# Two transformer blocks on one core: the router fed by the raw residual, and a new order of splits in the third block

## What is computed

```python
def memory_cross_attention(h, mem_n, ...):        # 4 heads of 256
    q = rms_norm_2((h @ w_cq).reshape(B, S, X_HEADS, X_HEAD_DIM), cq_norm)
    k = rms_norm_2((mem_n @ w_ck).reshape(B, M, X_HEADS, X_HEAD_DIM), ck_norm)
    v = (mem_n @ w_cv).reshape(B, M, X_HEADS, X_HEAD_DIM)
    p = jax.nn.softmax(scores, axis=-1)
...
def hierarchical_moe(h, w_router_group, w_router_expert, w1, w3, w2):
    p_group = jax.nn.softmax(xf @ w_router_group, axis=-1)     # 4 groups
    g_idx = jnp.argmax(p_group, axis=-1)
    local = jnp.einsum('td,gde->tge', xf, w_router_expert)     # 8 experts per group
    top_logit, top_idx = lax.top_k(local of the group, 2)
    gate = jax.nn.softmax(top_logit, axis=-1) * g_w[:, None]
    hid = jax.nn.silu(xblk @ w1[e]) * (xblk @ w3[e]); y = hid @ w2[e]    # 32 experts
...
    x = x + mixed @ w_out                          # mixed: window attention (8 heads) and a spatial gate
    x = x + memory_cross_attention(rms_norm_2(x, norm_cross), mem_n, ...)
    x = x + hierarchical_moe(rms_norm_2(x, norm_ffn), ...)
```

## Time and profile before

| | us |
|---|---|
| median of three executions | 1487.49 (1486.2 to 1488.25) |
| the profiled execution's own time | 1483.92 |
| span of the profile | 1481.9 |
| PE busy | 1437.8 (97%) |
| DVE busy | 755.2 (51%) |
| ACT busy | 565.2 (38%) |
| mean granted TensorE clock | 0.986 of full speed |

### The profile page before, as it was taken

One profiled execution on the slowest core, in us unless ns is written; L12 is line 12 of the kernel. 1 busy time (PEld: TensorE's weight loads), 2 busy tenths in 40 slices (PEclk: granted clock), 3 DMA queues, 4 the chain that ended last, 5 costly groups with the idle time before them and its releaser, 6 DMA issues. The chain is left out here.

```text
span 1481.9 us, 26323 instructions
## 1 busy us (share of the span) xinstructions
PE 1437.8 (97%) x11240; PEld 1211.5 (82%) x11240; DVE 755.2 (51%) x1194; ACT 565.2 (38%) x885; POOL 28.6 (2%) x47
## 2 busy tenths in 40 slices
PE   7999999999999999999999899999999999999997
PEld 4998899999999879999999789888666566566664
DVE  3968767876776656555555655644122122122121
ACT  2522235343454555444444664451212212212211
POOL 0100000000001010000000000010000000000000
PEclk9999999999999999999999999999999999999999
DMA  9996455979769514665645336426999999999996
GB/s 370 309 322 211 155 174 196 328 279 319 280 225 327 177 52 164 207 222 204 210 132 168 118 114 236 163 62 253 413 424 427 425 427 425 428 427 425 426 425 263
DMA packets 155378, 404.14 MB, mean 273 GB/s; under 512 B 5107, under 2 KB 123152, under 8 KB 133906
## 3 DMA queue, kind: packets, MB, share of 16 engines
q1 hardware_dynamic: 152960, 396.90, 71.1%
q0 software_dynamic: 1648, 5.18, 1.2%
q10 hardware_dynamic: 674, 0.64, 0.1%
HBM read 401.63 MB, written 1.07 MB: 272 GB/s over the span
## 5 line engine op out<-in xcount | busy, mean ns | idle before, releaser
L1999 PE MATMUL ps<-u,wsplit 128*128 128x256 f32 x3744 | 461.7, 284 | 5.3 <-DVE wsplit L1268 5.3
L1999 PEld LDWEIGHTS ps<-u,wsplit 128*128 128x128 f32 x3744 | 452.8, 192 | 11.9 <-DVE wsplit L1268 6.4
L1268 DVE TENSOR_TENSOR wsplit<-arena,wsplit 128x1024 fp32r<-128x1024 f32 x258 | 312.5, 1226 | 198.7 <-ACT wsplit L807 198.5
L807 ACT ACTIVATE wsplit<-arena 128x1024 fp32r<-128x1024 f32 x258 | 270.1, 1056 | 294.9 <-PE ps L1999 150.8
L2666 PE MATMUL ps<-arena 128*64 128x256 f32 x1408 | 155.9, 379 | 1.1 <-DVE arena L1897 0.8
L2666 PEld LDWEIGHTS ps<-arena 128*64 128x64 f32 x1408 | 101.6, 137 | 60.8 <-issue 12.6
L1902 DVE TENSOR_TENSOR arena<-arena,ps 128x256 f32<-128x256 f32 x32 | 13.5, 422 | 235.9 <-ACT arena L1216 223.8
L2261 PE MATMUL ps<-hid,wsplit 128*128 128x256 f32 x1056 | 130.7, 283 | 0.3 <-DVE hid L1524 0.3
L2261 PEld LDWEIGHTS ps<-hid,wsplit 128*128 128x128 f32 x1056 | 128.3, 192 | 0.5 <-DVE hid L1524 0.5
L1221 ACT ACTIVATE arena<-ps 64x512 f32<-64x512 f32 x62 | 36.6, 591 | 141.4 <-PE ps L2688 140.7
L2045 PE MATMUL ps<-wsplit,u 128*128 128x256 f32 x672 | 83.2, 284 | 1.8 <-ACT arena L1074 1.6
(11 more groups left out here) (369 smaller groups left out, 1376.3 us busy)
## 6 DMA issues: line engine op xcount, KB each, us to landing
arena<-in_w SPq DMA_DIRECT2D x64, 2048.0 KB, 22.4
late<-in_w SPq DMA_DIRECT2D x30, 2048.0 KB, 23.5
arena<-in_mod_w SPq DMA_DIRECT2D x48, 1024.0 KB, 7.0
arena<-in_ffn_w_in SPq DMA_DIRECT2D x44, 1024.0 KB, 5.9
arena<-in_ffn_w_out SPq DMA_DIRECT2D x22, 1024.0 KB, 5.0
arena<-in_a_w_in SPq DMA_DIRECT2D x16, 1024.0 KB, 8.6
arena<-in_kv_mod_w SPq DMA_DIRECT2D x8, 1024.0 KB, 4.9
arena<-in_kv_w SPq DMA_DIRECT2D x8, 1024.0 KB, 7.2
```

The source lines that it names most:

```text
L807: act.activation(piece_buf(p, 0), piece_src(p), ACT.Copy).then_inc(hi_done, 1)
L1268: dve.tensor_tensor(piece_buf(p, 1), piece_src(p), piece_buf(p, 0).bitcast(F32), ALU.subtract).then_inc(lo_done, 1)
L1999: mm = pe.matmul(o, w_[:, k, :], u[:, x_, k, :], start=first, stop=last)
```

## The change

Three things are altered.

1. **Router.** The router's weights go to `late`, 64 columns to a chunk (36 used, the rest zero), and are multiplied by the norm's weights on DVE (`m_gain`) between two steps of `co`. PE multiplies them by the raw residual, even chunks into partitions 0 to 63 of bank 6 and odd ones into 64 to 127 (`raw_logits`). DVE copies the sums to `log_t`, and PE adds the two halves and turns them by token in one product with `unite` (a doubled identity). DVE multiplies the 36 logits of each token by its reciprocal root.
2. **Tokens.** The scaled chunks and the permuted identity are gone. The residual is turned once, into banks 2 to 5, and stays there; ACT reads it from there, scales by the root and writes the tokens for the gather. The norm's weights (`token_gain`) are applied where DVE brings gathered tokens from PSUM to `xe`: a copy becomes a product.
3. **Order in the third block.** ACT writes the memory operand ahead of two of its other steps. In W, ACT goes head by head with one `between_w` behind each, and DVE puts a split between the steps of a pair. Three reciprocals of `key_norm` move into the additions of `out2`. In X, DVE does head 2's `probs` ahead of head 3's maxima and splits `co`'s pieces one by one.

The places on which the prediction rests, as each engine's instructions stand in the two kernels:

The diff, cut to its core:

```diff
+        wr = late[:, RING * SLOT:RING * SLOT + 64 * DC].rearrange("p (k e) -> p k e", k=DC)
+        token_gain = late[:, RING * SLOT + 512:RING * SLOT + 512 + DC]
+        unite = late[:, RING * SLOT + 520:RING * SLOT + 520 + NGROUP + NE]
+        log_t = late[:, RING * SLOT + 560:RING * SLOT + 560 + T]
...
-            pool.wait_ge(at_lo, 12)
-            pool.memset(turned, 0.0).then_inc(m_const, 1)
...
+            pool.wait_ge(at_s, HB + HW + HX)
+            pool.memset(wr, 0.0).then_inc(m_uni, 1)
+            pool.memset(unite, 0.0).then_inc(m_uni, 1)
+            pool.wait_ge(m_uni, 2)
...
+            pool.dma_start(token_gain, norm_ffn_2.rearrange("(p k) -> p k", k=DC)).then_inc(m_wr, 16)
...
+            pool.wait_ge(at_lo, 12)
...
+                    for i in range(n + 3):
+                        if i < n:
+                            exps(i)
+                        if 2 <= i < n + 2:
+                            copy(i - 2)
+                        if i >= 4 and i % 2 == 0:
+                            drain(i - 3)
+                        if i >= 1:
+                            between(i - 1)
...
                 hi_upto(min(FILL[0]["w"] + filled(min(i - 1, HW)) + 3, LAST["cv"] + 2))
-                while 2 * drained[0] + 2 <= min(filled(min(i - 1, HW)), 14):
+                while 2 * drained[0] + 2 <= min(filled(min(max(i - 1, 0), HW)), 14):
...
+                        hi_upto(pair[0]["w"] + LOOKAHEAD)
+                        memory_hi(pair[1]["w"])
...
+            def memory_hi(after):
...
+                act.wait_ge(x_tc, 2)
+                for c_ in range(DC):
+                    act.activation(u[:, 0, c_, :], memT[:, c_, :], ACT.Copy, scale=vec("norm_mem_2", c_))\
+                        .then_inc(u_hi, 1)
...
             in2_act()
-            wait_out(act, jobs["in2"][-1])
-            act.wait_ge(x_tc, 2)
-            for c_ in range(DC):
-                act.activation(u[:, 0, c_, :], memT[:, c_, :], ACT.Copy, scale=vec("norm_mem_2", c_)).then_inc(u_hi, 1)
...
+                    hi_upto(FILL[3]["w"])
+                    wait_out(act, jobs["in2"][-1])
...
+            act.wait_ge(rstd_done, STATS["moe"] + 1)
...
                 act.activation(
                     hn_tok[:, b, :].rearrange("p (k c q) -> p k c q", k=DC, c=DC),
-                    ps[:, 2 + 2 * b:4 + 2 * b, :].rearrange("p j (c k q) -> p k (j c) q", c=DC // 2, k=DC), ACT.Copy)\
-                    .then_inc(m_tokc, 1)
+                    ps[:, 2 + 2 * b:4 + 2 * b, :].rearrange("p j (c q k) -> p k (j c) q", c=DC // 2, k=DC), ACT.Copy,
+                    scale=stat[:, 4 + b:5 + b]).then_inc(m_tokc, 1)
...
+                    if job == "co" and n == 3:
+                        dve.wait_ge(m_wr, 96)
+                        routed = wr[:, :, 0:NGROUP + NE]
+                        gains = vec2[:, VEC["norm_ffn_2"]:VEC["norm_ffn_2"] + DC].rearrange("p (k o) -> p k o", o=1)
+                        dve.tensor_tensor(routed, routed, gains.to_broadcast([P, DC, NGROUP + NE]), ALU.mult)\
+                           .then_inc(m_gain, 1)
...
+                    if job == "out2" and n < 3:
+                        key_norm(n)
...
-                        if i == 1:
+                        if i in (1, 2):
                             probs(i)
...
-                        if i < n and i != 1:
+                        if i < n and i not in (1, 2):
...
+                    for j in range(n // 2):
+                        scores(2 * j)
+                        scores(2 * j + 1)
+                        if j == 0:
+                            split_first()
+                        probs(2 * j)
+                        if j > 0:
+                            between(2 * j - 1)
+                        probs(2 * j + 1)
+                        between(2 * j)
...
-            lo_upto(LAST["in2"] + LOOKAHEAD)
+            lo_upto(FILL[1]["w"])
...
+                    lo_upto(FILL[3]["w"])
...
+            attention_dve("W", None, between_w, lambda: lo_upto(FILL[2]["w"]))
...
                 lo_upto(p["w"] + LOOKAHEAD)
-                key_norm(n)
+                if n < 3:
+                    key_norm(3 + n)
...
-                lambda i: lo_upto(jobs["co"][(1, 3)[i]]["w"]) if i < 2 else None)
+                lambda i: lo_upto(jobs["co"][1 + i]["w"]) if i < 3 else None)
...
-            norm_rstd("moe")
-            for c_ in range(DC):
-                dve.scalar_tensor_tensor(out=sq[:, c_, :], in0=h[:, c_, :], scalar=vec("norm_ffn_2", c_), in1=rbc,
-                                         op0=ALU.mult, op1=ALU.mult).then_inc(m_hn, 1)
...
+            dve.wait_ge(bc_done, STATS["moe"])
...
+            dve.wait_ge(m_log, 1)
+            dve.tensor_copy(log_t, ps[:, 6, 0:T]).then_inc(m_log, 1)
...
-            dve.wait_ge(m_log, 1)
-            step(dve.tensor_copy(logits, ps[:, 6, 0:72].rearrange("p (b e) -> p b e", b=TB)))
...
+            step(*[dve.tensor_scalar(logits[:, b, :], ps[:, 6, T + 36 * b:T + 36 * (b + 1)], stat[:, 4 + b:5 + b], None,
+                                     ALU.mult) for b in range(TB)])
...
-                dve.tensor_copy(xe[:, 4 * half:4 * half + 4, :].rearrange("p k s -> p (k s)"), ps[:, 6 + half, :])\
-                    .then_inc(m_x, 1)
+                gains = token_gain[:, 4 * half:4 * half + 4].rearrange("p (k o) -> p k o", o=1)
+                dve.tensor_tensor(xe[:, 4 * half:4 * half + 4, :], ps[:, 6 + half, :].rearrange("p (k s) -> p k s", k=4),
+                                  gains.to_broadcast([P, 4, 2 * CAP]), ALU.mult).then_inc(m_x, 1)
...
+            def raw_logits(k):
+
+                half_ = 64 * (k % 2)
+                return pe.matmul(ps[half_:half_ + 64, 6, 0:T], wr[:, k, :], h[:, k, :], start=(k < 2), stop=(k >= DC - 2),
+                                 skip_group_check=True)
...
+            def residual(b, some):
+
+                for c_ in some:
+                    mm = pe.matmul(ps[:, 2 + 2 * b + c_ // 4, P * (c_ % 4):P * (c_ % 4 + 1)],
+                                   h[:, c_, P * b:P * (b + 1)], ident[:], start=(c_ % 4 == 0), stop=False,
+                                   skip_group_check=True)
+                if some[-1] == DC - 1:
+                    mm.then_inc(m_tok, 1)
...
+            pe.wait_ge(m_gain, 1)
+            for k in range(6):
+                raw_logits(k)
+            sums("moe", [3])
+            raw_logits(6)
+            raw_logits(7).then_inc(m_log, 1)
+            residual(0, range(2))
+            pe.wait_ge(m_log, 2)
+            pe.wait_ge(m_uni, 4)
+            for b in range(TB):
+                mm = pe.matmul(ps[:, 6, T + 36 * b:T + 36 * (b + 1)], log_t[:, P * b:P * (b + 1)], unite,
+                               start=True, stop=True, skip_group_check=True)
+            mm.then_inc(m_log, 1)
+            residual(0, range(2, DC))
+            residual(1, range(DC))
             warm(jobs["co"][4:], 3)
...
-            spread("moe")
...
-            for k in range(DC):
-                pe.wait_ge(m_hn, k + 1)
-                for b in range(TB):
-                    mm = pe.matmul(ps[:, 6, 36 * b:36 * (b + 1)], sq[:, k, P * b:P * (b + 1)], wr[:, k, :],
-                                   start=(k == 0 and b == 0), stop=(k == DC - 1), skip_group_check=True)
...
-            for b in range(TB):
-                for c_ in range(DC):
-                    mm = pe.matmul(ps[:, 2 + 2 * b + c_ // 4, P * (c_ % 4):P * (c_ % 4 + 1)],
-                                   sq[:, c_, P * b:P * (b + 1)], turned, start=c_ % 4 == 0, stop=c_ % 4 == 3)
-                mm.then_inc(m_tok, 1)
...
-            residual(0)
...
-            residual(1)
```

More of the change, by code:

```diff
@@ L608, in two_blocks @@
         slot_no = part(17920, 4, 2 * CAP)
-        wr = part(18432, DC, NGROUP + NE)
+        wr = late[:, RING * SLOT:RING * SLOT + 64 * DC].rearrange("p (k e) -> p k e", k=DC)
+        token_gain = late[:, RING * SLOT + 512:RING * SLOT + 512 + DC]
+        unite = late[:, RING * SLOT + 520:RING * SLOT + 520 + NGROUP + NE]
+        log_t = late[:, RING * SLOT + 560:RING * SLOT + 560 + T]
+        m_uni = sem("m_uni")
+        m_gain = sem("m_gain")
         logits = part(18720, TB, NGROUP + NE)
@@ L617, in two_blocks @@
         flag = part(19408, 4)
-        turned = part(17664, P)
         slot_i = part(19456, 4 * 2 * CAP)
@@ L1631, in attention_dve @@
                             drain(i - 2)
+                        between(i)
+                    return
+                if kind == "W":
+                    for j in range(n // 2):
[8 more added lines that the diff above has]
+                        between(2 * j)
+                    for i in (n - 1, n, n + 1):
                         between(i)
@@ L1751, in between_w @@
                 if i == 0:
+                    lo_upto(FILL[3]["w"])
+                    wait_out(dve, jobs["in2"][-1])
                     dve.wait_ge(w_std, 3)
```

45 lines of the change are left out of this document (20 added, 25 removed).

## The result

| | before | changed |
|---|---|---|
| median as first measured (4 executions each) | 1486.85 (1479.72 to 1488.25) | 1464.34 (1461.89 to 1465.26) |
| ratio, 95% interval | | 0.9856 (0.9822 to 0.9889) |
| the same kernel measured again | 1486.07 (9 executions) | 1466.51 (4), ratio 0.9865 (0.9849 to 0.9882) |
| mean of all executions timed with the experiments below | 1482.5 (83), mean clock 0.987 | with the first four: 1464.9 (8), mean clock 0.991 |
| span of the profile | 1481.9 | 1463.5 |

The change makes the kernel faster by 18 to 20 us, 1.2 to 1.4%: by the means over everything 1482.5 - 1464.9 is 17.7 (before rounding), by the means of the nine and four executions that ran side by side 19.6, by the medians 19.6 and 22.5. I had forecast 12.85, and 1474.6 with 1469.0 as the low end. The direction was right, the size was not.

A forecast was written before the change was run, and what follows sets the result against it. PE sets the pace before the experts, weights within them, so the end hangs on expert 0's start. 4.1 + 4.85 + 0.8 + 3.1 = 12.85 off 1483.92, plus 3.57 to the median: 1474.6 us, range 1469.0 to 1481.5.

The forecast's parts named there:

- What bounds the kernel: Weights pace the experts, PE the rest; time saved before expert 0 moves the end one to one, behind it 0.
- Window attention: Third block: earlier memory operand and splits shorten PE's pauses; 4.1 us after 1.5 off for one clock fall, bounds 1.5 to 6.0.
- Scores: Cross-attention: earlier keys' scaling removes the 1.89 pause, and 16 products take 3.8 instead of 6.76; 4.85 us.
- Turn of head 2: Cross-attention: division first cuts the wait from 2.13 to 1.4, half clock behind it kept; 0.8 us, bounds 0 and 2.6.
- Router: Logits 4.2 us sooner, 0.4 from the residual, less 1.5 for a half-clock gather; 3.1 us, bounds 2.2 and 5.2.
- The base: Sum taken from the profiled execution, 1483.92 us, with 3.57 added at the end to reach the median.
- The clock stays up everywhere: Rival: remaining pauses, 1.4 us or shorter, leave PE's clock up; gain 17.7, 1469.8. Gains above 15.5 got 0.17.
- Returned waits: Rival: window attention's pairs wait longer, scores gain only their pause; gain 7.3, 1480.2. Gains of 3 to 10 got 0.29.
- the change does what it says: Rival denied it: loads pace the query loop's split, so scores stay put; gain 8.0, 1479.5. Gains of 3 to 10: 0.29.
- Slower: Rival: odd heads' copies over 3 us late at four window attention outputs; 16 lost, +7 net, 1494; chance 0.04.
- GpSimd: Fills and selections moved beside divisions of heads 1 and 2: counted 0; by the skill's contention, sum some 0.5 us smaller.

The follow-up runs named there:

- e2: Kernel before with only three reciprocals of the keys' norm moved into the additions of out2: mean 1478.7 (12 executions), ratio 0.9968.
- e3: Kernel before with only head 2's division ahead of head 3's maxima and co's pieces split one by one: mean 1478.0 (12 executions), ratio 0.9970.
- e8: Kernel before with only window attention's memory operand and third and fourth split moved ahead, loops still by pairs of heads: mean 1478.1 (12), ratio 0.9975.
- e4: Kernel before with only the router and the tokens changed: mean 1479.3 (12 executions), ratio 0.9973.
- e12: Kernel before with four filling-product calls in the 1.89 us pause ahead of cross-attention's scores: mean 1480.1 (12) beside 1482.5 (23), ratio 0.9980.
- e6: Changed kernel with three filling products ahead of each of window attention's two gates: 121.74 us from the start of the third block to out2.
- e13: Changed kernel with ACT's split of co's fourth piece behind head 2's exponentials, plus one filler call ahead of each gate: 120.21 us from block start to out2.

## Why the prediction was off

*What bounds the kernel* was right: the end hangs on expert 0's start, the half of the residual taken from behind it gave nothing, and the pauses that were named and the router are where the time came from. The time came out 10 us lower than forecast. About 5 of that is the base, some 4 are the four terms, and two steps in them failed: what I gave back in window attention, and the price of the half clock, which I read off one profile at every place.

*Window attention, 4.1 forecast, 7.4 measured.* Of the terms this one failed most. Up to the gates the walk was right: 3.0 forecast, and they stand 63.11 us behind the start of the block instead of 66.09. Then I gave back 0.45 for the drains, 1.0 at the first outputs and 0.6 at the copies; none of these came, and the pauses alone gave 6.4 in place of 4.2 (5.6 less the 1.4 of clock in it). The remaining 1.0 is clock. I expected it to fall once as before. It does, but in four of the six old profiles it falls twice, behind the pause of 1.39 and also behind that of 2.36, which the new order takes away; I had read the one stretch of my own profile as the rule. PE timeline of e2, the split's pause, where 24 products took 3.14 in my profile:

```profile
833.97 4.64 PE L2002 MATMUL ps<-u,wsplit 128*128 128x256 f32 x24 [2.36 <-DVE wsplit L1268]
```

*Scores, 4.85 forecast, 3.7 measured.* The pause was right (2.0). The half clock behind it costs 3.0, 1.7, 1.7, 1.7, 1.7 and 0.0 in the six profiles that have the pause, 1.6 on average. I had taken the 3 us of the worst one, my own, as its price.

*Turn of head 2, 0.8 forecast, 1.7 measured.* The wait went as forecast (2.13 to 1.47), 0.7 of the 1.7. The rest is clock: with the old order the half clock follows in five of eight profiles, with the new one in none of eight, and I had kept it. My reason, the fall behind the 1.39 at 845.02, didn't carry: the new order has a fall just ahead of that turn without any pause there.

*Router, 3.1 forecast, 4.3 measured.* DVE's first use of the logits comes 3.7 sooner after the last product of co, not 4.2, and the gather starts 4.2 sooner (17.46 us behind it before, 13.27 now), where 4.6 was forecast; at equal clock, e3's 21.73 against 17.87, the path gave 3.9. I took off 1.5 for a half clock in the gather as if it came always. It came in four of seven profiles; and the old order had falls of its own, which cost 3.2 in three of eight and up to 0.4 in the others.

*The base.* I set my sum against the median of three, 1487.49, which lies 5 above the mean of 83 executions. The 3.57 us that I added for the way from the profiled execution to the median was scatter: the means of before by round go from 1481.7 to 1485.4. This is half of the miss in time, and it was bad luck in the draw as much as a wrong step. By the segments' 16.5 from 1482.5 the time would be 1466.0, and 1464.9 was measured.

*The rivals.* "The clock stays up everywhere" comes nearest in size (17.7), but not by its mechanism: the clock still falls at the gates and, at times, in the gather. What it missed is that the old kernel's falls are more than one profile shows. Returned waits are what e8 alone has (3.44 for 1.39); with the order by heads they don't come. The keys' scaling was paced by DVE, as the pause that is gone in e2 shows, so that the change does what it says. Slower was out of reach: the copies of the odd heads were late at one place by 0.96, where 1.34 had stood.

*GpSimd.* In the changed kernel its transfers' set-up stands beside the division of head 2, and the two halves of that take longer than in e3, where GpSimd is idle. DVE and POOL timeline of the changed kernel, then DVE of e3:

```profile
959.46 0.85 DVE L1650 TENSOR_SCALAR arena<-arena,small 128x256 f32<-128x256 f32 x2
```

```profile
959.06 3.50 POOL L789 DMA_DIRECT2D late<-in_w_router_expert  x4
```

```profile
969.04 0.62 DVE L1612 TENSOR_SCALAR arena<-arena,small 128x256 f32<-128x256 f32 x2
```

That is 0.23 us, and the wait at the turn is 1.47 against e3's 1.23. In all eight profiles with the new router one or two such pairs take 0.81 to 1.04, in the eight with the old one none takes over 0.62. DVE timeline of e4, where the order of the heads is the old one and the wait at the turn is 2.34 instead of 2.13:

```profile
975.09 0.81 DVE L1629 TENSOR_SCALAR arena<-arena,small 128x256 f32<-128x256 f32 x2
```

The Trainium skill (GPSIMD Engine Reference, 1. Specifications) limits the contention for the shared SBUF interfaces to VectorE's instructions in a 2-port mode or with two SBUF inputs, a condition that I had left out. The traces agree with it in that these divisions get slower; which of the two cases they are, no run here shows. The price is half of the 0.5 that I had put beside it without a row. No run moved GpSimd's work alone.

## What to carry to other kernels

Read a stretch at half clock in one profile as one draw: ask for several executions, or profiles of kernels that share the place, before it gets a price. Take a gain first by the path alone (pauses, at equal clock), then give the clock a term of its own with both ends open; here the two were 13 and some 4 us. A split moved ahead pays only if the engine that makes it isn't late with what is wanted next: of two reorderings of 1.5 and 2.5 us apiece the pair was worth 6.4. And set a sum against the mean of many executions, not a median of three.

## What the runs showed that I had not expected

The granted clock falls to half (1.2 GHz) for stretches that cost 1.4 to 1.7 us, or about twice that. It falls behind pauses of PE of 1.3 to 2.4 us and, at the gates, without a pause just ahead; behind most of these pauses it falls in some profiles only (1.89: five of six; 2.13: five of eight). Of identical code ahead of the third block the start differs by up to 5.1 us between profiles. Over all executions of before the time goes from 1476.5 to 1489.0, and the mean clock with it. The Trainium skill (TensorE: Matmul & The Clock Gate, Part 1) says that what watches the engine's activity runs freely and is not tied to the kernel's start; that agrees with these draws at the same place, though no run here shows the mechanism.

Filling a pause with products without a use may be worth 1 to 2 us without shortening any wait (e12, with an interval that all but reaches nothing), but where the filler itself is in the path it about pays for itself (e6, e13).
